# Gathers of expert rows run five selections ahead of the dots instead of three

## What is computed

```python
def _peer(tok, wq, subkeys, u_tab, v_tab):
    def chunk(hc):                                     # 128 tokens
        q = (hc @ wq).reshape(PEER_CHUNK, PEER_HEADS, 2, PEER_DK // 2)
        s = jnp.einsum('chpd,hpnd->chpn', q, subkeys)
        ...                                            # two top-16 lists, their 256 sums, top-16 of these -> sc, e
        g = jax.nn.softmax(sc, axis=-1)
        a = jax.nn.gelu(jnp.einsum('chkd,cd->chk', u_tab[e], hc), approximate=False)
        return jnp.einsum('chk,chkd->cd', g * a, v_tab[e])
```

## Time and profile before

| | |
|---|---|
| median of 3 runs | 5437.69 us (5434.0 to 5438.31) |
| the profiled execution's own time | 5433.36 us |
| its span in the profile | 5431.3 us |
| busy: PE / DVE / POOL / ACT | 69% / 61% / 37% / 37% of the span |
| data moved by DMA | 1532 MB, 1342 MB of it by the 1280 gathers |
| mean granted TensorE clock | 0.81 of full speed |
| selections 520 to 767 beside layer 1's first stages | about 2673 to 3590 us of the span |

### The profile page before, as it was taken

The page is one execution under the profiler, slowest core; times in us unless marked ns, Lnnn a source line. Parts: engine busy times, 40 slices in busy tenths (PEclk is TensorE's granted clock), DMA queues, the critical chain, the costliest instruction groups (busy, mean ns, idle before and its releaser), DMA issues. The chain is left out here.

```text
span 5431.3 us, 59703 instructions
## 1 busy us (share of the span) xinstructions
PE 3760.0 (69%) x19504; PEld 1838.0 (34%) x19504; DVE 3330.3 (61%) x7026; ACT 1988.8 (37%) x5136; POOL 2036.3 (37%) x1533
## 2 busy tenths in 40 slices
PE   6899879987565555555577679678976555555554
PEld 3677338876111111111122245246852111111111
DVE  7622452223777777777687777764135777777776
ACT  5432002212443344343354444325223443343443
POOL 5112003212444444444483356211434444444443
PEclk8999989998767777777688889889988777777777
DMA  5012002212999999999998989841327999999998
GB/s 237 16 44 70 4 16 65 63 67 103 400 418 410 416 410 417 415 414 414 378 363 349 367 327 375 349 171 37 98 80 325 421 412 417 413 415 416 411 417 345
DMA packets 230644, 1532.43 MB, mean 282 GB/s; under 512 B 26164, under 2 KB 26740, under 8 KB 58044
## 3 DMA queue, kind: packets, MB, share of 16 engines
q0 software_dynamic: 184320, 1342.26, 60.5%
q1 hardware_dynamic: 46012, 186.36, 9.4%
HBM read 1515.31 MB, written 13.21 MB: 281 GB/s over the span
## 5 line engine op out<-in xcount | busy, mean ns | idle before, releaser
L536 PE MATMUL psum<-arena 64*64 64x512 f32 x10240 | 1769.8, 825 | 1220.8 <-ACT arena L515 1209.6
L491 POOL DMA_INDIRECT arena<-in_uv,arena x1280 | 1462.9, 1143 | 1817.7 <-PE psum L536 1392.6
L651 DVE SCALAR_TENSOR_TENSOR arena<-arena 128x1024 f32<-128x1024 f32 x1280 | 1621.4, 1267 | 697.8 <-DMA arena<-in_uv,arena 653.0
L536 PEld LDWEIGHTS psum<-arena 64*64 64x64 f32 x10240 | 418.1, 169 | 2519.8 <-ACT arena L515 1892.9
L1549 PE MATMUL psum<-view_at,view_at 128*128 128x512 f32 (+1 forms) x4896 | 966.5, 359 | 19.1 <-PEq L165 10.3
L504 ACT ACTIVATE arena<-arena 128x1 f32<-128x1 f32 x1280 | 258.2, 202 | 1850.8 <-DVE arena L651 1811.0
L265 POOL TENSOR_TENSOR view_at<-view_at,view_at 128x1024 fp32r<-128x1024 f32 (+1 forms) x192 | 455.2, 2380 | 1238.7 <-ACT view_at L299 1208.4
L1549 PEld LDWEIGHTS psum<-view_at,view_at 128*128 128x128 f32 x4896 | 815.3, 191 | 185.2 <-issue 54.4
L515 ACT ACTIVATE arena<-arena 128x64 f32<-128x64 f32 x1280 | 445.1, 348 | 52.7 <-PE psum L536 10.9
L508 ACT ACTIVATE arena<-arena 128x1 f32<-128x1 f32 x1280 | 376.9, 294 | 46.7 <-ACT arena L504 0.4
L299 ACT ACTIVATE view_at<-view_at 128x1024 fp32r<-128x1024 f32 (+1 forms) x176 | 163.9, 939 | 330.6 <-DMA view_at<-in_w_in 188.2
(11 more groups left out here) (246 smaller groups left out, 3445.6 us busy)
## 6 DMA issues: line engine op xcount, KB each, us to landing
view_at<-in_w_in SPq DMA_DIRECT2D x108, 512.0 KB, 6.6
view_at<-in_w_mod SPq DMA_DIRECT2D x48, 1024.0 KB, 12.9
arena<-in_uv,arena POOLq DMA_INDIRECT x1280
view_at<-in_w_br SPq DMA_DIRECT2D x48, 256.0 KB
view_at<-in_w_out SPq DMA_DIRECT2D x16, 512.0 KB, 8.7
view_at<-in_wq SPq DMA_DIRECT2D x16, 512.0 KB, 3.4
arena<-mod_rows SPq DMA_DIRECT2D x12, 512.0 KB
keep_spectrum<-arena SPq DMA_DIRECT2D x18, 256.0 KB, 6.9
```

The lines of the kernel that those rows point to most:

```text
L491: nc.gpsimd.indirect_dma_start(out=self.slots[i % self.ring], out_offset=None, in_=self.table, in_offset=bass.IndirectOffsetOnAxis(ap=self ...
L536: last = nc.tensor.matmul(self.c.psum[tokens, at:at + 512], self.diag[rows, k % 4], self.slots[k % self.ring][rows, D + h * 512:D + (h + 1 ...
L651: nc.vector.scalar_tensor_tensor(out=self.junk, in0=self.slots[i % self.ring][:, 0:D], scalar=1.0, in1=self.h2_turned if i % 2 else self.h ...
```

## The change

The class constant `FETCH` goes from 3 to 5, and `EARLY` from 4 to 2, so that their sum, the selections gathered at the end of `phase_query`, stays 7.

```diff
-    SUM_LAG, FETCH = 2, 3
+    SUM_LAG, FETCH = 2, 5
...
-    EARLY = 4
+    EARLY = 2
```

## The result

| | before | after |
|---|---|---|
| median of 14 runs each, same chip, us | 5436.44 (5431.65 to 5442.24) | 5445.02 (5436.62 to 5453.2) |
| ratio, 95% interval | | 1.0017 [1.001, 1.0024] |
| span of the profiled execution, us | 5431.3 | 5444.5 |

The forecast was 5438 and no change. It came out 0.17% slower: just inside the 0.2% that I had called no change, but the interval excludes both a gain and zero. This small number is made of two large ones.

What follows compares the result with a forecast made beforehand. DMA was taken as full where experts run alone, so the change could act only in 2673 to 3590 us. Mod +14, conv -8, hand-overs -3 and -3 sum to 0: 5438 us, no change, range 5420 to 5456.

Steps and rivals of the forecast that it cites:

- Mod, +14: Mod stage: POOL's gathers wait for sums of their own step and delay its splits; 14 us longer, bounds +20 and -5.
- I take half of it, 5: Mod stage: earlier landings save half of PE's 9.5 us wait for ACT's rounding, 5 us against 19.3 lost.
- Conv, -8: Conv stage: two selections more in flight close gaps in DMA; 8 us saved, bounds 0 and PE's 23.1.
- Hand-overs, -3 and -3: Starts of conv and of the ten experts alone: two selections already gathered before the barrier; 3 us saved at each.
- Elsewhere ... 0 each, within 2 us ... DVE or SP end later: Spectrum and long conv stages: no change, since the extra gathers at a stage's end finish before DVE or SP.
- The load loses at most half of the engines however deep the other queue is: Mod's 1 MB weight loads: engines take packets from queues in turn, so deeper gathers add nothing to the loads' landing.
- Faster, mod pays nothing: Rival: mod stays at 0, conv takes all idle DMA time; -18 us, 5420; chance 0.27.
- Slower: Rival: mod's whole 19 us of POOL wait come, conv gives only 3; +16, 5454; chance 0.25.
- A dot gets ahead of a split: Mod stage: earlier dots hold POOL's 12 splits by 1.2 us each, 15 at most; left at nothing, within the slower 0.25.
- No effect: Rival: the ring of eight slots limits mod and conv too, both unchanged, 5438; chance 0.48 together with the sum.
- Loads later: Mod's weight loads land 5.4 us later behind two more gathers, 43 us; taken as nothing, part of the slower case.

Runs made afterwards that it cites:

- e_mod: Kernel before with five ahead in the mod stage alone, three everywhere else and in mod's last step; 5456.5 us, 1.0043 of before.
- e_split: The change, but in mod GpSimd (POOL) splits the next odd block before the even step's gathers; 5420.3 us, 0.9977 of before.
- e_four: Four ahead everywhere instead of the change's five (`FETCH` 4, `EARLY` 3); 5417.6 us, 0.9975 of before.
- e_start4: e_mix with three ahead in mod's first step too; 5412.7 us, 0.9963 of before.
- e_start5: e_start4 with five ahead instead of four in mod's inner steps and the GpSimd order of e_split; 5410.3 us, 0.996 of before.
- e_conv: Kernel before with five ahead in the conv stage alone, three everywhere else; 5417.0 us, 0.9971 of before.
- e_trim: The change, with three ahead in the last step of mod and of both spectra; 5434.5 us, 1.0 of before.
- the mixed kernels: e_mix and e_start4, both with four ahead in mod, three in the spectra, five from norm1 on; 5407.5 and 5412.7 us.
- e_mix: Four ahead in mod (three in its last step), three in spectra, five from norm1 on, GpSimd's order unedited; 5407.5 us, 0.9955 of before.
- e_late: Three ahead in mod and both spectra as before, five from norm1 on; 5415.1 us, 0.9965 of before.

## Why the prediction was right and wrong

That the total was close is in part luck, since two errors met: the gains were 17.2 us where I had 14, the losses 27.3 where I had 14. The miss in the losses, 13.3 us, is alone more than the 10.9 that I had called no change.

- **Mod, +14: mis-sized, measured +20.4.** The mechanism stands (e_mod, e_split). Cut at POOL's splits, the 20.4 us are 3.7 from the stage's start to the first split, 16.0 from there to the last one, and 0.7 behind it. Between the splits the 14 was near. POOL waited 33.9 us for sums where I had 24.9 of new wait, and "I take half of it, 5" for the earlier landings can't be read from the change, whose ACT waited for weights instead (62.9 us). Where the waits are gone it came: 150.8 us between the splits in e_split and 150.6 in e_four, against 156.5 before. What failed is the stage's start, for which the sum has no term: the first weight block lands 2.5 us later, behind gathers already queued, and with three ahead in the first step it lands in time (e_start4, e_start5).
- **Conv, -8: right.** e_conv alone gives 8.4. The DMA share of 0.99 and DVE's waits under 20 came as forecast.
- **Hand-overs, -3 and -3: right, somewhat small.** Measured were some 4 and, over the runs with five ahead in conv, 4.3 to 5.8.
- **"Elsewhere ... 0 each, within 2 us ... DVE or SP end later": wrong, +6.9.** I named SyncE as ending later and gave it no price: I looked for what stands behind the last gather on POOL. SyncE ends the stage, and its last store now meets a full queue of gathers; from the store's issue to the barrier it is 3.2 and 2.4 us more in the spectra. e_trim shows it. In mod the same costs 2.2 us, which are within its 20.4.
- **"The load loses at most half of the engines however deep the other queue is"**: near enough for the loads of 1 MB in mod on average (7.6 us before, 8.1 after), and used too narrowly. What counts for a short transfer is how much of the gathers is still to move when it is issued: with three ahead in the last step of a spectrum 0.3 to 1.0 MB were, with five 2.6.
- **Rivals.** *Faster, mod pays nothing* fell as stated; its 5420 is what e_split measured, but by another order on POOL. *Slower* was right on mod (20.4 for its 19) and wrong on conv, which did not give only 3. *A dot gets ahead of a split*: a split takes 4570 ns instead of 4730, the dots 1448 instead of 2107, so nothing of it came. Its row was also misread: the dot of 5.50 us ends at 2815.30, not just behind the split (2812.99) but 1.1 us behind the instruction that POOL runs next (L752, 2812.93 to 2814.20), as if it waited for both. *No effect* fell: mod and conv both moved. *Loads later* fell with e_mod and e_split.
- Mod with four ahead took 186.9 us once, and 193.0 and 190.5 in the mixed kernels. The splits from first to last agree (150.6, 151.5 and 152.0). The first split came 20.6, 24.5 and 21.4 us after the stage's start, which explains 3.9 of the 6.1 us in e_mix and 0.8 of the 3.6 in e_start4; 1.4 and 1.3 lie behind the last split. Each is one profiled execution, and why the last part differs is not shown. Nor was it tried to issue the stage's last store from another queue.

## What to carry to other kernels

A constant that says how far ahead to fetch is a property of a stage, not of the kernel. Before raising it, count for each stage how many requests then need something that the same step produces, and look at what stands behind them on the issuing engine. The count alone doesn't decide: it is 24 of 36 in mod, which lost, and 62 of 74 in conv, which gained. If work that another engine waits for stands behind them, move that work ahead of the request, raise the number by one only, or leave the stage as it was (e_late), which did as well here. Where a stage ends with a small store that something waits for, let the queue of large transfers run nearly dry ahead of it.

## What the runs showed of the hardware

A store of 256 KB issued with 2.6 MB of gathers still to move had no packet moved for 3.4 us, then shared the engines, and its last packet came 6.6 to 6.8 us after the issue (both spectrum stages, after and e_split). With 0.65 MB or less of gathers left it started at 0.8 us and was done at 3.6 (first spectrum) or 4.2 to 4.3 (second). Two stores of mod rows, 24 KB each, show the same, before and after, in the DMA view (KB, median us to landing):

```profile
mod_rows<-arena SPq DMA_DIRECT2D x2, 24.0 KB, 1.5
```

```profile
mod_rows<-arena SPq DMA_DIRECT2D x2, 24.0 KB, 3.7
```

And the first weight block of mod, 1 MB, landed 2.5 us later with the change.

The price grows with what is left of the gathers, up to a limit. These are the last stores of the two spectrum stages, 28 in 14 runs, counted from the packets of the traces:

| gathers still to move at the issue, MB | stages | first packet of the store, us behind the issue |
|---|---|---|
| 0.3 to 0.65 | 16 | 0.8 |
| 0.75 to 1.0 | 6 | 1.1 to 1.9 |
| 1.5 (e_four, first) | 1 | 2.9 |
| 2.1 (e_four, second) | 1 | 3.4 |
| 2.6 (after, e_split) | 4 | 3.4 or 3.5 |

So four ahead pays nearly what five pays in the spectra: 7.1 and 7.9 us from the issue to the barrier. SyncE's queue at the end of the first spectrum stage in e_four:

```profile
2977.69 0.32 SPq L2063 DMA_DIRECT2D keep_spectrum<-arena  x1
2984.95 0.25 SPq L2053 DMA_DIRECT2D arena<-in_hy_bias  x1
```

In mod four ahead pays nothing of it: under 0.05 MB of gathers were left at the last store, and it is 2.5 us (e_four) and 2.3 (e_mix) to the barrier, as with three. What is left is not all that counts: in mod with five ahead 0.9 MB were left, and the stores' first packet came 2.5 us behind the last issue.
